# Computing the query projection by seven Strassen products, two of them ahead of the key/value strip

## The reference

```
h = rmsnorm(x, attn_norm_g)
proj = h @ w_in        # columns: conv B | conv C | conv x | q (1024) | k, v (128 each) | gate_conv | gate_attn
y_conv = (u_b * short_conv(u_c * u_x, conv_w)) @ w_conv_out
attn = sliding_window_attention(q, k, v, sinks, rel_bias)     # 16 heads of 64, blocks of 128 tokens
y_attn = attn @ w_attn_out
mixed = sigmoid(g_conv) * y_conv + sigmoid(g_attn) * y_attn
x = x + mixed @ w_o
x = x + square(relu(rmsnorm(x, mlp_norm_g) @ w_up)) @ w_down
out = rmsnorm(x, final_norm_g)
```

## Time and profile before

| | us |
|---|---|
| median of 3 runs | 757.71 (757.30 to 758.04) |
| the profiled execution: its own time | 757.86 |
| the span in its trace | 756.1 |
| granted TensorE clock over the span | 0.997 of full speed |

### The profile page before, as it was taken

How to read it: one execution, slowest core, us unless ns; L and a number is a source line. 1 busy time by engine, 2 the same in 40 slices (tenths; PEclk the granted TensorE clock), 3 DMA queues, 4 the chain that set the end, 5 groups by cost and what they waited for, 6 DMA issues and landing times.

```text
span 756.1 us, 10473 instructions
## 1 busy us (share of the span) xinstructions
PE 745.3 (99%) x4067; PEld 646.6 (86%) x4067; DVE 646.3 (85%) x748; ACT 419.8 (56%) x535; POOL 81.9 (11%) x117
## 2 busy tenths in 40 slices
PE   8999999999999999999999999999999999999996
PEld 7888888888888888888878899889988999899985
DVE  5766688889899686989899999998799879986997
ACT  7424555453644656664548776654465355545555
POOL 3202000121112101001000101010101010000102
PEclk9999999999999999999999999999999999999998
DMA  7727513143237996766965746767677767676703
GB/s 256 248 83 279 168 55 112 57 108 114 72 123 223 293 263 169 222 166 187 301 180 138 222 142 168 211 178 193 190 175 190 200 168 207 183 198 191 196 1 112
DMA packets 69408, 131.22 MB, mean 174 GB/s; under 512 B 2604, under 2 KB 22132, under 8 KB 69364
## 3 DMA queue, kind: packets, MB, share of 16 engines
q1 hardware_dynamic: 50400, 84.18, 33.4%
q0 software_dynamic: 18752, 46.15, 27.6%
q10 hardware_dynamic: 212, 0.28, 0.1%
HBM read 124.29 MB, written 6.32 MB: 173 GB/s over the span
## 4 chain that ended last, share of the span: by engine, by line
PE 90%; DVE 4%; DMA 3%; issue 2%; ACT 1%; SPq 0%; DVEq 0%; ACTq 0%
PE pair L959 38%; PE pair L918 21%; PE pair L727 8%; PE pair L729 8%; PE pair L728 8%; DMA home_raw<-in_w_attn_out 2%; PE pair L774 2%; DVE home_lo L1756 1%; PE pair L749 1%; PE pair L748 1%; PE pair L758 1%; DMA xn<-in_x 1%; PE pair L820 1%; DVE mixed L1948 0%; DVE s_lo_tile L1812 0%
## 5 line engine op out<-in xcount | busy, mean ns | idle before, releaser
L1191 ACT ACTIVATE high<-home_raw 128x2048 fp32r<-128x2048 f32 x91 | 174.3, 1915 | 147.3 <-PE pair L959 96.7
L1756 DVE TENSOR_TENSOR home_lo<-home_raw,high 128x2048 fp32r<-128x2048 f32 x91 | 208.4, 2290 | 37.2 <-ACT high L1191 36.8
L959 PE MATMUL pair<-high,s_hi_tile 128*128 128x512 f32 x440 | 110.3, 391 | 0.0
L959 PE MATMUL pair<-high,s_lo_tile 128*128 128x512 f32 x440 | 110.0, 390 | 0.1
L959 PE MATMUL pair<-home_lo,s_hi_tile 128*128 128x512 f32 x440 | 109.3, 389 | 0.0
L727 PE MATMUL pair<-h,wgt 128*128 128x512 f32 x256 | 101.5, 397 | 0.0
L729 PE MATMUL pair<-h,wgt 128*128 128x512 f32 x256 | 99.9, 390 | 0.0
L728 PE MATMUL pair<-h,wgt 128*128 128x512 f32 x256 | 99.8, 390 | 0.0
L959 PEld LDWEIGHTS pair<-high,s_lo_tile 128*128 128x128 f32 x440 | 82.4, 188 | 17.6 <-DVE s_lo_tile L1812 0.5
L959 PEld LDWEIGHTS pair<-home_lo,s_hi_tile 128*128 128x128 f32 x440 | 82.5, 188 | 17.1
L959 PEld LDWEIGHTS pair<-high,s_hi_tile 128*128 128x128 f32 x440 | 81.8, 188 | 17.2 <-ACT pair L1283 0.5
(11 more groups left out here) (215 smaller groups left out, 1001.8 us busy)
## 6 DMA issues: line engine op xcount, KB each, us to landing
raw<-in_w_in SPq DMA_DIRECT2D x34, 512.0 KB, 4.6
home_raw<-in_w_up SPq DMA_DIRECT2D x16, 1024.0 KB, 5.5
home_raw<-in_w_down SPq DMA_DIRECT2D x16, 1024.0 KB, 5.1
home_raw<-in_w_up POOLq DMA_DIRECT2D x12, 1024.0 KB, 8.3
home_raw<-in_w_down POOLq DMA_DIRECT2D x12, 1024.0 KB, 8.3
home_raw<-in_w_in POOLq DMA_DIRECT2D x7, 1024.0 KB, 8.3
home_raw<-in_w_in SPq DMA_DIRECT2D x7, 1024.0 KB, 6.5
home_raw<-in_w_conv_out SPq DMA_DIRECT2D x4, 1024.0 KB, 5.1
```

The lines of the kernel that those rows point to most:

```text
L959: last = mm(pair[region(s, i)][:, b, :], a_[:, k, b * P:(b + 1) * P], w[:, k, :], start=(fresh and kind == 0 and k == 0), stop=(kind == 2 ...
L1191: a(high[n % 2][:, :], home_raw[home_of(s, name)][:, :], ACT.Copy).then_inc(m_hi, 1)
L1756: v.tensor_tensor(home_lo[home][:, :], home_raw[home][:, :], f32(high[n % 2][:, :]), ALU.subtract).then_inc(m_lo, 1)
```

## The change

The four query strips are replaced by the seven Strassen products over the same operands (`q_product`, 48 matmuls of 256 columns each, 336 in all). M1 and N2 use only the first 256 tokens, so they are placed in front of the key/value strip, and x is transposed, scaled and split in two halves of 256 tokens; the transposes of the late half stand inside N2. ACT writes the late half's high part a second time, unsplit, into `qa`. T3 and T1 of q are each a plain load and an accumulating transfer, T4 is an accumulating transfer onto T2, T2 a sum on DVE. Two details elsewhere: the load of WO's B12 waits for T1 of AO to be complete (`t1_in`) instead of for its first block (`t1_base`), and DVE does `s4(AO)` before `low_part(AO, M6)` instead of after it.

```diff
+            load_x(0)
+            load_x(1)
+            load_q_half(M1, 0, 0, q_b11[0])
+            load_q_half(M1, 0, 1, q_b11[1])
+            load_x(2)
+            load_x(3)
+            load_q_half(N2, 1, 0, q_b21[0])
+            load_q_half(N2, 1, 1, q_b21[1])
             load_t(S_KV, 0, 0, w_in, COL_KV)
+            load_q(M7, 0, 1, q_t3_base)
+            sp.wait_ge(xt_ready, 8)
+            load_q(M5, 0, 0, q_t1_base)
+            sp.wait_ge(lo_ready, 2)
+            load_q(M3, 1, 1, q_b22)
...
-            sp.wait_ge(t1_base, 16 * (AO + 1))
+            sp.wait_ge(t1_in, 16 * (AO + 1))
             load_block(WO, 0, 1)
...
+            pool.wait_ge(q_t3_base, 16)
+            add_q(M7, 1, 1, q_t3_in)
...
+            pool.wait_ge(q_t1_base, 16)
+            add_q(M5, 0, 1, q_t1_in)
...
+            def q_product(i, between={}):
...
+                for kind in range(3):
+                    w, a_ = ((whi, ahi), (whi, alo), (wlo, ahi))[kind]
...
+                        last = mm(acc[:, f, :], w[:, k, f * P:(f + 1) * P], a_[:, k, :],
...
-            first_strip()
+            q_product(M1)
+            q_product(N2, {1: late_transposes})
+            kv_strip()
+            pe.wait_ge(q_c11_base, 1)
...
-            with pe.Fori(0, 2) as i:
-                it = Pass(i, 0, 2)
-                transposed_strip(S_Q, 2, it, 1, 2, h)
-                transposed_strip(S_Q + 1, 2, it, 2, 2, h)
+            q_product(M6)
+            q_product(M5)
+            pe.wait_ge(q_c12_base, 1)
+            q_product(M7)
             value_transposes()
+            pe.wait_ge(q_c22_base, 1)
+            q_product(M3)
+            pe.wait_ge(q_c22, 1)
+            q_product(N4)
+            pe.wait_ge(q_c11, 1)
...
+            def tile_high(half, at_, k):
+
+                act.wait_ge(xt_ready, 4 * half + k % 4 + 1)
+                gain_ = pcol[:, g1 + k:g1 + k + 1]
+                t = cols(2 * P * half, 2 * P)
+                a(h[:, 0, k, t], tile_of(k), ACT.Copy, scale=gain_).then_inc(h_hi if not half else wide, 1)
+                if half:
+                    a(qa[:, k, t], tile_of(k), ACT.Copy, scale=gain_).then_inc(h_hi, 1)
...
+            def q_high_part(i):
...
+                act.wait_ge({M6: q_t2, M5: q_t1_in, M7: q_t3_in, M3: q_b22, N4: q_t4_in}[i], 1 if i == M6 else 16)
+                act.wait_ge(q_prod, 2 * (at_ - 2) + 2)
+                a(q_hi[at_ % 2][:, :], q_raw[i][:, :], ACT.Copy).then_inc(q_high, 1)
...
+            def q_sum_t2():
+                dve.wait_ge(q_t3_in, 16)
+                v.tensor_tensor(q_raw[M6][:, :], q_raw[M1][:, :], q_raw[M7][:, :], ALU.add).then_inc(q_t2, 1)
...
+            h_s3()
+            h_s2()
+            q_sum_t2()
+            sum_low(M6)
+            h_s1()
+            q_low_part(M6)
...
             gate_conv(2)
+            s4(AO)
             low_part(AO, M6)
-            s4(AO)
             gate_attn(0)
```

More of the change, by code:

```diff
@@ L789, in _ @@
             idle_transposes(28)
[L790 to L795, removed]
+            x_transposes(0)
             pe.wait_ge(rows_in, 16 * 3)
             nc.tensor.transpose(bank[KT - 1][:, T - 5 * KT:T], prow[:, :], ident[0:5 * KT, 0:5 * KT]).then_inc(par_t, 1)
-            idle_transposes(2)
-            pe.wait_ge(xn_ready, 3)
@@ new lines, in late_transposes, with kv_strip @@
+            def late_transposes():
+                pe.wait_ge(h_ready, 8)
+                x_transposes(2)
+                x_transposes(3)
+            def kv_strip():
+                w = wgt[weight_slot(S_KV)][:, :, :].rearrange("p c (k n) -> p c k n", k=KT)
+                for j in range(2):
+                    for at_, k in enumerate(LATE_TILES):
+                        if j == 0:
+                            pe.wait_ge(lo_ready, k // 4 + 1)
+                            pe.wait_ge(h_ready, 8 + max(at_, 2) + 1)
+                        half = cols((1 - j) * P, P)
+                        wh, wl = w[:, 0, k, half], w[:, 1, k, half]
+                        first, end = at_ == 0, at_ == KT - 1
+                        acc = bank[B_KV + j][:, :]
+                        mm(acc, wh, h[:, 0, k, :], start=first, stop=False)
+                        mm(acc, wh, h[:, 1, k, :], start=False, stop=False)
+                        last = mm(acc, wl, h[:, 0, k, :], start=False, stop=end)
+                    last.then_inc(half_ready[j], 1)
@@ L1094, in _, with root @@
             a(rms[:, 0, 0:1], eps[:, :], ACT.Sqrt)
-            for b in range(TB):
+            def root(b):
                 act.wait_ge(x_in[b], 16)
@@ new lines, in sum_high, with q_copy @@
+            def sum_high(i):
+                act.wait_ge(hs_step, {M7: 2, M6: 3, M5: 5, M3: 7}[i])
+                k = HS.index(i)
+                a(hs_hi[k][:, :, :], hs_sum[k][:, :, :], ACT.Copy).then_inc(hs_split, 1)
+            def q_copy(i, j, of, done, scale=1.0):
+                act.wait_ge(q_prod, 2 * Q_ORDER.index(of) + 2)
+                if i:
+                    act.wait_ge(hs_step, 3)
+                a(four_of(qa, i, j), four(Q_REGION.get(of, 3))[:, :, :], ACT.Copy, scale=scale).then_inc(done, 1)
@@ L1543, in lo_chunks, with scale_x @@
                                     f32(w[:, 0, 1024 * e:1024 * e + 1024]), ALU.subtract).then_inc(lo_ready, 1)
-            for b in range(TB):
+            def scale_x(b):
                 dve.wait_ge(root_done, b + 1)
@@ new lines, in _ @@
+            dve.wait_ge(par_t, 1)
+            v.tensor_copy(pcol[:, :], bank[KT - 1][:, T - 5 * KT:T]).then_inc(par_ready, 1)
+            q_low_half(M1, 0)
+            for k in range(4):
+                tile_low(0, k, k)
+            q_low_half(M1, 1)
+            scale_x(2)
+            for k in range(4, 8):
+                tile_low(0, k, k)
+            q_low_half(N2, 0)
+            q_low_half(N2, 1)
+            scale_x(3)
+            lo_chunks(S_KV)
+            for at_, k in enumerate(LATE_TILES):
+                tile_low(1, at_, k)
```

359 lines of the change are left out of this document (219 added, 140 removed).

## The result

| | before | after |
|---|---|---|
| median, us | 757.66 (757.30 to 758.04, 4 runs) | 762.78 (762.41 to 763.14, 4 runs) |
| ratio | | 1.0068, 95% interval 1.0050 to 1.0085 |
| the profiled execution, its span | 757.86, 756.1 | 762.49, 760.8 |

The kernel became slower by 5.1 us where 1.7 had been forecast (759.4); the measured median lies 0.6 above the range. In the profiled executions it is +4.6.

The account below looks back on a forecast made before the run. TensorE was taken as the bound, nine tenths of the chain. 757.86 - 1.3 (query stage) + 3.0 (AO and WO) = 759.6, 759.4 on the median's scale; own range 758.2 to 761.0, with rivals 755.0 to 762.2.

Parts of the forecast that it names:

- The mechanism and the sign: AO and WO: holding back B12 delays T3 of WO, outweighing the query stage's gain; forecast 759.4 us, slower.
- the length of T3 of WO beside other loads: Stage WO: accumulating transfer beside B11 and B21 takes 13.4 to 14.5 us, landing at 379.2 to 380.3.
- the high end: AO and WO: residual and T1's base also lengthen T3, up to 3 us each, partly after it is done: +5.
- The term of +3.0: AO and WO: T3 of WO lands late against 376.86 and DVE's sum waits; +2.4 to +3.4 us, +3.0 taken.
- The issue time: Stage WO: with B12 issued at 360.5 and landing at 365.6, T3's second block leaves at 365.8.
- DVE's own gain: AO into WO: DVE would reach the sum T2 of WO at 375.8 instead of 376.86, -1.0 us.
- What PE would wait for: AO and WO: PE waits 4 to 5 us in total for `mixed` and `zc`, where it waited 1.6.
- The query stage, in the profiled execution: Up to the mixer: M1 at 10.9, 1 to 2 us wait before M6, mixer near 67.2; gain 1.3 us.
- the case, T3 of q between 29.7 and 35.9: Query stage: T3 at 35.9 or a longer ACT-DVE chain makes it lose, +1.5 there, 762.2 overall; chance 0.14.
- the statement that later stages only move: Later stages: PE runs without gaps, so they only shift in time; same distances as before up to AO.
- Rival 1: AO and WO: held-back B12 costs nothing, T3 of WO in time by 376.86; 755.7 or 754.7 us, chance 0.28.
- The matmuls: Query products: 336 matmuls of 256 columns at 0.120 us take 40.3 us instead of 43.5, -3.2 us.

Follow-up runs that it names:

- res: Changed kernel with the residual's first load moved behind WO's B22 load; 761.19 us, ratio 1.0053.
- wait: Kernel before with one edit, the load of WO's B12 waiting for `t1_in` instead of `t1_base`; 763.6 us, ratio 1.0080.
- before_early_2: Kernel before with the `s4` swap, WO's B12 loaded during CO, T1's base of WO held until B21 landed, residual's first load behind B22; 757.00 us.
- base: Changed kernel with the load of WO's B12 waiting for `t1_base` again; 757.72 us, ratio 1.0009.
- both: Changed kernel with the old B12 wait and the old `s4(AO)` order, so only the query stage differs from before; 757.79 us, ratio 1.0009.
- early: Changed kernel with WO's B12 loaded ahead, during stage CO, instead of held back; 757.59 us, ratio 1.0007.
- kv: **base** with q's T3 base loaded ahead of the key/value weights; 756.94 us, ratio 0.9993.
- q22: **base** with q's B22 loaded only after T1 of q has landed; 757.74 us, ratio 1.0003.
- best: **q22** together with **early**, the residual's first load moved behind B22 and T1's base of WO held until B21 landed; 756.27 us, ratio 0.9984.

## Why the prediction was wrong, step by step

- **The mechanism and the sign were right, the size of one term was wrong.** The step that failed is the length of T3 of WO beside other loads. The prediction said 13.4 to 14.5 us in flight ("T3 lands at 379.2 to 380.3"), for two plain loads, and put the residual only into the high end. Two loads and the residual made 15.4 to 15.9; **res** has 12.95 without the residual. So the two loads that were priced cost 4.7 where 5.1 to 6.2 had been put, and the one left out of the middle value cost 3.0. The term of +3.0 measured +5.3 (**wait**) to +6.5 (after), and +3.6 in **res**: the nearness of that one to the forecast is in part luck, since a later issue made up for the shorter length.
- **The issue time.** T3 was to leave at 365.8; it left at 366.4 in **wait**, and at 365.36 on a clock 1.9 us ahead in after, that is 367.3. B12 was priced rightly (5.1; 5.43 and 4.88), T1's second block at 8.3 took 8.63 and 8.54, and T1's base, kept at its 7.38, took 8.73 in after. That is another 0.6 to 1.5 us.
- **DVE's own gain** of 1.0 (375.8 instead of 376.86) was right: 376.0 in **before_early_2**, on a clock 0.2 behind. So was the statement that nothing between the sum T2 and the merges takes a delay up (19.9 us for 19.8).
- **What PE would wait for** was right: 4 to 5 us for `mixed` and `zc` predicted, 6.3 measured.
- **The query stage, in the profiled execution**: M1 at 10.58 for 10.9, 0.8 in front of M6 for 1 to 2, the mixer at 66.6 for 67.2, the gain 1.9 for 1.3. Each of these stood within 0.6. It was also a favourable draw: of the executions with this query stage and these loads about 3 in 10 go the other way.
- **The query stage at the median** was wrong in another way: **base** and **both** are equal to before. The prediction had the case, T3 of q between 29.7 and 35.9 with PE losing all of it, and gave it 0.14 as a way the kernel might be; it is a way that single executions go, some 3 in 10 of them above 760.5. Its price also lacked the clock: +1.5 was forecast, and the mixer of **early** came 2.8 late. And the statement that later stages only move was wrong for AO, which takes 0.7 to 0.8 back with the old order of loads.
- **Rival 1** (equal turns, T3 of WO in time) was wrong: 7.5 us of waiting for it. At T3 of q in after the 11.0 and 10.2 us do look like equal turns, and it landed at 32.05, near the 32.4 of that rival.
- **The high end** of the AO and WO term, +5, had been reached by adding "up to 3 us each, partly after T3 is done". The range should have held the sum with every load that is in flight at full price.
- **The matmuls** were right: 96 of 256 columns took 11.51 to 11.78 us in after (0.120 to 0.123 each). The 109 ns that the prediction sets against this are the gap of an isolated matmul: the Trainium skill (TensorE: Matmul & The Clock Gate, Back-to-back issue gap) says that its formula under-counts at small widths in a stream of weight loads and matmuls. The 120 ns of the earlier trace rows agree with that.

## What to carry to other kernels

Before a load is held back for the sake of a neighbour, follow the whole chain that begins with it: here block, sum by transfer, sum on DVE, low part and merges, and a transfer that had 8 us to spare became the last to arrive. Count as company of a slow transfer everything that is issued before it lands, not only what is issued with it. When a load disturbs another, first look for an earlier place for it, where the engines idle, and only then for a later one.

If a needed transfer lands within a microsecond or two of its use, one profiled execution says little: look at the spread of the times, and profile one of the upper ones too. And when gains don't add up, compare the distance between two fixed instructions in both traces, stage by stage, before testing further edits.

## What the runs showed of the hardware that was not expected

- An accumulating transfer of 1 MB took 8.2 to 8.8 us with little beside it, 10.2 to 11.6 in most cases beside one or two plain loads and 13.1 to 14.1 in some, 12.95 beside two in stage WO, 15.4 to 15.9 beside three. In **kv** T3 of q took 8.7 though two plain loads joined it half-way.
- A plain load issued behind an accumulating transfer in POOL's queue did not visibly slow it: 15.4 us with the load held back, 15.9 and 15.45 with it behind.
- The same pair of transfers went 11.0 and 10.2 us in one execution and 14.1 and 6.1 in another.
- One load at one place in the program (T1's base of AO) took 7.36 to 7.54 us in the five profiled kernels with the old query stage and 8.65 to 8.85 in the twelve with the new one; the cause is not known.
- PE's idling of 4.3 us was followed by 5 us at clock 0.52; that of 5.9 by eight matmuls at twice their time; a wait of 2.3 us in front of M5 once by a lower clock (**both**: 0.70 to 0.73 for 6 us, 13.25 us for 96 matmuls), and a wait of 2.3 or 2.4 us at the same place twice not (**q22**: 11.78; **best**: 1.00).
